# A gated feed-forward on one NeuronCore: the up-projection's 640 tokens split 512 + 128 over two PSUM banks, in place of 320 + 320

## The chip, the core and the metric

The kernel runs on one core of a Trainium2 chip. The metric is the device time of one execution in microseconds, lower is better. A core has TensorE (PE, with a matmul part and a weight-load part, PEld, that overlap), VectorE (DVE), ScalarE (ACT), GpSimd (POOL) and SyncE (SP, which here only issues DMAs). Matmul results land in PSUM, which has 8 banks of 512 f32 values per partition; one matmul writes into one bank.

## The reference

The program is a two-layer streaming encoder over 512 prompt tokens and 8 running streams with 16 new tokens each, 640 tokens in all. After the attention part, each layer ends in a gated feed-forward:

```
def _conv_ffn(x, conv_hist, w_up, conv_w, conv_b, w_down):
    u = x @ w_up
    a, b = u[..., :D_FF], u[..., D_FF:]
    a_ext = jnp.concatenate([conv_hist.astype(a.dtype), a], axis=1)
    a_conv = lax.conv_general_dilated(a_ext, conv_w[:, None, :].astype(a.dtype), (1,), 'VALID',
                                      dimension_numbers=('NWC', 'WIO', 'NWC'),
                                      feature_group_count=D_FF) + conv_b
    h = jax.nn.gelu(a_conv, approximate=False) * b
    return h @ w_down, a_ext[:, -(CONV_W - 1):]
```

The model width is 1024, D_FF is 2816, and the convolution has 3 taps along time. The prompt starts with an empty history; each of the 8 streams has its own history of 2 rows, and returns its last 2 rows. So the convolution treats the 512 prompt tokens as one run and the 128 stream tokens as 8 runs of 16.

## The kernel before, in words

Features lie on the partitions and the T = 640 tokens on the free dimension (HT = 320 is half of them, SEQ = 512, TS = 128). All weights come as slabs of up to 2048 columns, two slabs in flight. Precision comes from a split of every operand into a rounded high part and a low part of the type float32r, and each product is three matmuls: high x high, low x high, high x low.

- SyncE loads a slab into `w_raw`. ScalarE rounds it to `w_hi` (line 551), GpSimd subtracts to get `w_lo` (line 471).
- TensorE works in numbered *jobs*. A job is one 128-feature output tile for all 640 tokens; it owns two PSUM banks, and four jobs are in flight (8 banks). `dense` (lines 1131 to 1149) is a job over `tiles` contraction tiles: for each tile and each of the three products, two matmuls with the same weights, one for each half of the tokens. `four` (lines 1158 to 1177) runs four jobs together, tile by tile, as the layer norm before it delivers `x_lo`; it is used at the head of the input projection and at the head of the up-projection. The matmuls are recorded at line 1147 (`dense`) and line 1174 (`four`), those of the helper `full` with plain f32 at line 1155.
- `up_half` (lines 1395 to 1401) is the up-projection: a loop over slabs, each with one job for a tile of `a` and one for the same tile of `b`. It runs 10 slabs after `four` took the first two, then `down_half` works off 12 tiles, then `up_half` runs the other 10 slabs, and the last down-projection follows, with the layer norm.
- ScalarE's `feed` (lines 691 to 711) copies an `a` tile from PSUM into `f_ext`, the prompt after two zero columns, and each stream after its two history columns, and saves the new history in `tail`. VectorE's `feed` (lines 1048 to 1067) does the three taps into `f_conv`, ScalarE the gelu, VectorE the product with the `b` tile in PSUM into `f_h`, and the two split the result into `hf_hi` and `hf_lo`, from which `down_half` reads.

The order is written out by hand for each engine; semaphores (`job_done`, `job_taken`, `whi_ready`, `wlo_ready`, `fh_lo_ready` and others) hold the engines together. The inner loop of `dense`:

```
for x, w in ((hi, wh), (lo, wh), (hi, wl)):
    for a in range(2):
        ins = MM(out_[:, a, :], w, x[:, t, a * HT:(a + 1) * HT],
                 start=t == 0 and w is wh and x is hi, stop=t == tiles - 1 and w is wl)
```

Of the kernel before, what the change touches and what calls it, by code (L numbers as in the profile page):

```python
# [28 lines left out]
ALU = mybir.AluOpType  # L29
ACT = mybir.ActivationFunctionType  # L30
# [3 lines left out]
DEPTH, D, SEQ, NREQ, TDEC, PAST, CHUNK, WINDOW = 2, 1024, 512, 8, 16, 512, 64, 128  # L34
TS = NREQ * TDEC
T = SEQ + TS
HT = T // 2
KD = D // P
# [29 lines left out]
S_UP1 = S_OUT + 4  # L68
# [11 lines left out]
J_UP1 = J_OUT + KD + 3  # L80
# [51 lines left out]
def build(nc, inp, out):  # L132
    ctx = ExitStack()
    with ctx:
# [4 lines left out]
        x_hi = sb("x_hi", [P, KD, T], F32R)  # L139
        x_lo = sb("x_lo", [P, KD, T], F32R)  # L140
# [8 lines left out]
        tail = sb("tail", [P, NF, (NREQ + 1) * (CW - 1)])  # L149
# [95 lines left out]
        f_ext = place("f_ext", 12 * T, [P, EXT + 2])  # L245
        f_conv = place("f_conv", 12 * T + EXT + 2, [P, EXT + 2])
        f_gelu = place("f_gelu", 12 * T + 2 * (EXT + 2), [P, EXT + 2])
        assert 3 * (EXT + 2) <= 4 * T
        hf_lo = place("hf_lo", 24 * T, [P, F1, T], F32R)
        f_h = place("f_h", 36 * T, [P, T])  # L250
# [6 lines left out]
        ps = ctx.enter_context(nc.psum_tensor("ps", [P, 8, 512], F32))  # L257
# [48 lines left out]
        def pair(n, parts=slice(0, P)):  # L306
            k = 2 * (n % 4)
            return ps[parts, k:k + 2, 0:HT]

        def flat(bank, n, parts=slice(0, P)):  # L310

# [26 lines left out]
        def row(t, j):  # L338

            if isinstance(j, int):  # L340
                return t[:, j, :]
            return t[:, bass.ds(j, 1), :].rearrange("p a n -> p (a n)")
# [186 lines left out]
        def _(act):  # L529
            A = act.activation  # L530
            for k in range(KD):
                act.wait_ge(x_loaded[k // 2], 16)
                A(x_hi[:, k, :], x_in[:, k, :], ACT.Copy).then_inc(xn_hi, 1)
                if k in (1, 3):
                    s = k // 2
# [5 lines left out]
            with act.Fori(0, DEPTH) as layer:  # L541
# [149 lines left out]
                def feed(j, k, jj, job0, n_first, ahead):  # L691

                    act.wait_ge(job_done, layer * NJ + JC + n_first + 2 * jj + 1)
                    act.wait_ge(conv_ready, layer * NF + j + 1)
                    ahead(k, (0,))
                    a = pair(job0)
                    A(f_ext[:, 2:2 + HT], a[:, 0, :], ACT.Copy)
                    A(f_ext[:, 2 + HT:2 + SEQ], a[:, 1, 0:SEQ - HT], ACT.Copy)
                    streams = f_ext[:, 2 + SEQ:EXT].rearrange("p (r n) -> p r n", r=NREQ)
                    A(streams[:, :, 2:], a[:, 1, SEQ - HT:].rearrange("p (r n) -> p r n", r=NREQ), ACT.Copy)  # L700
                    A(streams[:, :, 0:2], row4(hist, j), ACT.Copy)
                    A(row(tail, j)[:, 0:2], a[:, 1, SEQ - HT - 2:SEQ - HT], ACT.Copy)
                    A(row(tail, j)[:, 2:].rearrange("p (r n) -> p r n", r=NREQ),  # L703
                      a[:, 1, SEQ - HT:].rearrange("p (r n) -> p r n", r=NREQ)[:, :, TDEC - 2:], ACT.Copy
                      ).then_inc(ext_ready, 1)
                    act.wait_ge(conv_ready, layer * NF + j + 2)
                    act.wait_ge(fh_ready, layer * NF + j + 1)
                    A(f_gelu[:, 0:NC_], f_conv[:, 0:NC_], ACT.Gelu).then_inc(gelu_ready, 1)  # L708
                    ahead(k, (1,))
                    act.wait_ge(fh_ready, layer * NF + j + 2)  # L710
                    A(row(hf_hi, jj), f_h[:], ACT.Copy).then_inc(fh_hi_ready, 1)  # L711
# [32 lines left out]
        def _(dve):  # L744
# [13 lines left out]
            TT, TSC, STT = dve.tensor_tensor, dve.tensor_scalar, dve.scalar_tensor_tensor  # L758
# [10 lines left out]
            with dve.Fori(0, DEPTH) as layer:  # L769
# [19 lines left out]
                for q in range(4):  # L789
                    ins = TT(kr_r[32 * q:32 * q + 32, :], kr_t[:, 0, :], kr_t[:, 1, :], ALU.add)  # L790
# [47 lines left out]
                for k in range(2):  # L838
# [6 lines left out]
                    for q in range(4):  # L845
                        ins = dve.tensor_copy(q_rs[:, :, 4 * k + q, :],
                                              q_r[32 * q:32 * q + 32, k, SEQ:].rearrange("p (r n) -> p r n", r=NREQ))
# [199 lines left out]
                def feed(j, jj, job0, n_first):  # L1047
                    w = lambda c: vec[:, bass.ds(V_CW + c * NF + j, 1)]
                    dve.wait_ge(ext_ready, layer * NF + j + 1)
                    dve.sem_inc(job_taken, 1)  # L1050
                    link(TSC(f_conv[:, 0:NC_], f_ext[:, 2:EXT], w(2), vec[:, bass.ds(V_CB + j, 1)], ALU.mult, ALU.add))  # L1051
                    link(STT(f_conv[:, 0:NC_], f_ext[:, 1:EXT - 1], w(1), f_conv[:, 0:NC_], ALU.mult, ALU.add))
                    STT(f_conv[:, 0:NC_], f_ext[:, 0:EXT - 2], w(0), f_conv[:, 0:NC_], ALU.mult, ALU.add  # L1053
                        ).then_inc(conv_ready, 1)
                    dve.wait_ge(job_done, layer * NJ + JC + n_first + 2 * jj + 2)
                    dve.wait_ge(gelu_ready, layer * NF + j + 1)
                    up = pair(job0 + 1)
                    TT(f_h[:, 0:HT], up[:, 0, :], f_gelu[:, 0:HT], ALU.mult)
                    TT(f_h[:, HT:SEQ], up[:, 1, 0:SEQ - HT], f_gelu[:, HT:SEQ], ALU.mult)
                    link(TT(f_h[:, SEQ:].rearrange("p (r n) -> p r n", r=NREQ),  # L1060
                            up[:, 1, SEQ - HT:].rearrange("p (r n) -> p r n", r=NREQ),
                            f_gelu[:, SEQ + 2:EXT].rearrange("p (r n) -> p r n", r=NREQ)[:, :, 0:TDEC], ALU.mult))
                    dve.sem_inc(fh_ready, 1)
                    dve.sem_inc(job_taken, 1)
                    dve.wait_ge(fh_hi_ready, layer * NF + j + 1)
                    TT(row(hf_lo, jj), f_h[:], row(hf_hi, jj).bitcast(F32), ALU.subtract).then_inc(fh_lo_ready, 1)  # L1066
                    dve.wait_ge(fh_lo_ready, layer * NF + j + 1)
# [41 lines left out]
        def _(pe):  # L1109
            MM = pe.matmul  # L1110
# [6 lines left out]
            with pe.Fori(0, DEPTH) as layer:  # L1117
# [9 lines left out]
                    pe.wait_ge(whi_ready, layer * (2 * NS) + (2 * s + half + 1) + i * (2 * sper))  # L1127
                    pe.wait_ge(wlo_ready, layer * (2 * NS) + (2 * s + half + 1) + i * (2 * sper))

                def dense(n, s, tile0, tiles, hi, lo, part=None, i=0, jper=0, sper=0, ready=None):  # L1130

                    start_job(n, i, jper)
                    if part is not None:
                        weights(s, part % 2, i, sper)
                    out_ = pair(n)
                    for t in range(tiles):
                        if part == 2 and t == tiles // 2:
                            weights(s, 1, i, sper)  # L1140
                        if ready is not None:
                            ready(t)
                        c = (tile0 + t) * P
                        wh, wl = w_hi[:, s % 2, c:c + P], w_lo[:, s % 2, c:c + P]
                        for x, w in ((hi, wh), (lo, wh), (hi, wl)):
                            for a in range(2):
                                ins = MM(out_[:, a, :], w, x[:, t, a * HT:(a + 1) * HT],  # L1147
                                         start=t == 0 and w is wh and x is hi, stop=t == tiles - 1 and w is wl)
                    ins.then_inc(job_done, 1)

# [4 lines left out]
                        ins = MM(out_[:, a, :], lhs, rhs[:, a * HT:(a + 1) * HT], start=first, stop=last)  # L1155
                    return ins

                def four(n, s, before):

                    for k in range(4):
                        start_job(n + k)

                    for t, slot in [(0, 0)] + [(t + 1 - slot, slot) for t in range(KD - 1) for slot in (0, 1)] + [(KD - 1, 1)]:
                        pe.wait_ge(xn_lo, before + t + 1)
                        for j in (2 * slot, 2 * slot + 1):
                            if t == 0:
                                weights(s + slot, j % 2)
                            out_ = pair(n + j)
                            c = (j % 2 * KD + t) * P  # L1170
                            wh, wl = w_hi[:, slot, c:c + P], w_lo[:, slot, c:c + P]
                            for x, w in ((x_hi, wh), (x_lo, wh), (x_hi, wl)):
                                for a in range(2):
                                    ins = MM(out_[:, a, :], w, x[:, t, a * HT:(a + 1) * HT],  # L1174
                                             start=t == 0 and w is wh and x is x_hi, stop=t == KD - 1 and w is wl)
                            if t == KD - 1:
                                ins.then_inc(job_done, 1)
# [217 lines left out]
                def up_half(s0, job0, n):  # L1395
                    settle(pe)
                    with pe.Fori(0, n) as i:
                        for k in range(2):
                            g = dict(i=i, jper=4, sper=2)
                            dense(job0 + 2 * k, s0 + k, 0, KD, x_hi, x_lo, 0, **g)  # L1400
                            dense(job0 + 2 * k + 1, s0 + k, KD, KD, x_hi, x_lo, 1, **g)

                def rows(t, f0):
                    pe.wait_ge(fh_lo_ready, layer * NF + (f0 + t + 1))
# [5 lines left out]
                            dense(job0 + k, s0 + k, 0, nf, hf_hi, hf_lo, 2, i=i, jper=4, sper=4,  # L1410
                                  ready=(lambda t: rows(t, 0)) if k == 0 else None)

                four(J_UP1, S_UP1, layer * (2 * KD) + KD)
                up_half(S_UP1 + 2, J_UP1 + 4, F1 // 2 - 1)
                down_half(S_DN1, J_DN1, F1)
                up_half(S_UP2, J_UP2, F2 // 2)
# [147 lines left out]
```

## Time and profile before

| | us |
|---|---|
| median of 2 runs | 2218.32 (2212.05 and 2224.59) |
| span of the profiled execution, first to last instruction | 2210.7 |
| PE busy in it | 2066.8 (93%) |
| DVE, ACT, POOL busy | 974.5, 649.3, 679.4 |

### The profile page before, as it was taken

The page shows a single profiled execution, that of the slowest core. Times are in us where ns is not written, and L with a number is a line of the kernel's source. Part 1 is how long each engine was busy: PE and PEld are TensorE (multiplying, and loading weights), DVE is VectorE, ACT ScalarE, POOL GpSimd, SP SyncE. Part 2 cuts the span into 40 slices and gives each one's busy share as a digit, 9 for nine tenths or more (in the row PEclk, how much of TensorE's full clock was granted, in tenths as well). Part 3 has the DMA queues.
Part 4 walks back from the last instruction along what each step waited for, and adds up shares of the span by engine and source line. Part 5 has one row for each costly group of instructions (what it writes and reads, how often), then busy time and mean ns, then how long its engine had stood idle before and what let it go on. Part 6 is the DMA issues. An engine that isn't in the chain of part 4 may idle for free.

```text
span 2210.7 us, 33980 instructions
## 1 busy us (share of the span) xinstructions
PE 2066.8 (93%) x12730; PEld 1892.0 (86%) x12730; DVE 974.5 (44%) x1437; ACT 649.3 (29%) x1267; POOL 679.4 (31%) x328
## 2 busy tenths in 40 slices
PE   6888999999989999999989889999998999999993
PEld 5774666999979999999989557689997999999992
DVE  3457444221656432343364764532147544234336
ACT  2213223322235321332231232233322433123322
POOL 2320000233624334432732100013345333343265
PEclk9897589999989999999999777999999999999997
DMA  5220011122212212211231101102221121221121
GB/s 145 107 91 0 33 33 51 58 72 83 73 39 95 71 58 83 93 69 48 79 119 57 48 13 42 62 29 77 80 80 58 61 92 57 76 79 73 55 79 71
DMA packets 36662, 148.56 MB, mean 67 GB/s; under 512 B 6488, under 2 KB 11384, under 8 KB 28344
## 3 DMA queue, kind: packets, MB, share of 16 engines
q1 hardware_dynamic: 36568, 147.30, 19.7%
q8 instruction: 60, 0.98, 0.2%
q14 instruction: 34, 0.28, 0.0%
HBM read 141.34 MB, written 7.78 MB: 67 GB/s over the span
## 4 chain that ended last, share of the span: by engine, by line
PE 77%; issue 13%; POOL 5%; DVE 4%; ACT 1%; DMA 0%; POOLq 0%; SPq 0%; DVEq 0%; ACTq 0%
PE ps L1147 59%; POOL w_lo L471 4%; PE ps L1281 2%; PE ps L1261 2%; PE ps L1258 2%; PE ps L1323 2%; PE ps L1268 1%; PE ps L1313 1%; PE ps L1240 1%; PE ps L1267 1%; PE ps L1327 1%; POOL sum_sq L495 1%; PE ps L1260 1%; ACT probs L586 1%; PE ps L1318 0%
## 5 line engine op out<-in xcount | busy, mean ns | idle before, releaser
L471 POOL TENSOR_TENSOR w_lo<-w_raw,w_hi 128x1024 fp32r<-128x1024 f32 (+3 forms) x268 | 581.2, 2182 | 1509.9 <-ACT w_hi L551 1499.0
L1147 PE MATMUL ps<-x_hi,w_hi 128*128 128x320 f32 x2016 | 462.3, 311 | 27.2 <-POOL w_lo L471 27.2
L1147 PE MATMUL ps<-x_hi,w_lo 128*128 128x320 f32 x2016 | 461.1, 310 | 0.0
L1147 PE MATMUL ps<-x_lo,w_hi 128*128 128x320 f32 x2016 | 461.0, 310 | 0.0
L551 ACT ACTIVATE w_hi<-w_raw 128x1024 fp32r<-128x1024 f32 (+3 forms) x264 | 239.0, 924 | 526.7 <-PE ps L1147 500.8
L1147 PEld LDWEIGHTS ps<-x_hi,w_hi 128*128 128x128 f32 x2016 | 338.8, 189 | 29.2 <-ACT w_hi L551 21.4
L1147 PEld LDWEIGHTS ps<-x_lo,w_hi 128*128 128x128 f32 x2016 | 338.8, 189 | 0.0
L1147 PEld LDWEIGHTS ps<-x_hi,w_lo 128*128 128x128 f32 x2016 | 338.6, 189 | 0.0
L1051 DVE TENSOR_SCALAR f_conv<-f_ext,vec 128x656 f32<-128x656 f32 x44 | 66.2, 1506 | 226.9 <-ACT tail L703 224.1
L1147 PE MATMUL ps<-hf_hi,w_hi 128*128 128x320 f32 x704 | 160.8, 309 | 0.0
L1147 PE MATMUL ps<-hf_hi,w_lo 128*128 128x320 f32 x704 | 160.3, 308 | 0.0
L1147 PE MATMUL ps<-hf_lo,w_hi 128*128 128x320 f32 x704 | 160.3, 308 | 0.0
L1147 PEld LDWEIGHTS ps<-hf_hi,w_hi 128*128 128x128 f32 x704 | 117.6, 188 | 0.3
L1147 PEld LDWEIGHTS ps<-hf_hi,w_lo 128*128 128x128 f32 x704 | 117.6, 188 | 0.0
L1147 PEld LDWEIGHTS ps<-hf_lo,w_hi 128*128 128x128 f32 x704 | 117.6, 188 | 0.0
L1066 DVE TENSOR_TENSOR hf_lo<-f_h,hf_hi 128x640 f32 x44 | 83.1, 1889 | 46.5 <-ACT hf_hi L711 46.5
L1174 PE MATMUL ps<-x_hi,w_hi 128*128 128x320 f32 x256 | 62.9, 329 | 38.4 <-DVE x_lo L1000 30.0
L958 DVE TENSOR_TENSOR mix_b<-ps,gate_b 128x640 f32<-128x640 f32 x16 | 13.2, 824 | 155.7 <-PE ps L1147 155.7
L1174 PEld LDWEIGHTS ps<-x_hi,w_hi 128*128 128x128 f32 x256 | 46.0, 203 | 41.5 <-issue 40.2
L708 ACT ACTIVATE f_gelu<-f_conv 128x656 f32<-128x656 f32 x44 | 33.1, 752 | 162.4 <-DVE f_conv L1053 162.4
L1281 PEld LDWEIGHTS ps<-ident,probs 128*128 128x128 f32 (+1 forms) x384 | 49.4, 158 | 36.5 <-issue 17.8
L1281 PE MATMUL ps<-ident,probs 128*128 128x128 f32 (+1 forms) x384 | 70.7, 323 | 8.9 <-DVE probs L900 8.9
(215 smaller groups left out, 3052.9 us busy)
## 6 DMA issues: line engine op xcount, KB each, us to landing
w_raw<-in_slabs SPq DMA_DIRECT2D x64, 1024.0 KB, 4.8
w_raw<-in_slabs SPq DMA_DIRECT2D x52, 768.0 KB, 4.1
w_raw<-in_slabs SPq DMA_DIRECT2D x16, 640.0 KB, 3.8
ckvc<-in_ckvc SPq DMA_DIRECT2D x16, 256.0 KB, 2.6
ckvc_t<-in_ckvc_t SPq DMA_DIRECT2D x16, 256.0 KB, 2.8
x_in<-in_x_t SPq DMA_DIRECT2D x4, 640.0 KB, 8.6
out_y_t<-res SPq DMA_DIRECT2D x8, 320.0 KB, 2.1
bias_p<-bias_table SPq DMA_DIRECT2D x2, 1024.0 KB, 7.9
```

The costliest lines, as they stand in the source:

```text
L471: pool.tensor_tensor(w_lo[:, s % 2, c], w_raw[:, s % 2, c], w_hi[:, s % 2, c].bitcast(F32), ALU.subtract).then_inc(wlo_ready, 1)
L495: pool.tensor_tensor(sum_sq[:], sq[:, 0, :] if k == 1 else sum_sq[:], sq[:, k % 2, :], ALU.add).then_inc(added_sq, 1)
L551: A(w_hi[:, s % 2, c], w_raw[:, s % 2, c], ACT.Copy).then_inc(whi_ready, 1)
L708: A(f_gelu[:, 0:NC_], f_conv[:, 0:NC_], ACT.Gelu).then_inc(gelu_ready, 1)
L1051: link(TSC(f_conv[:, 0:NC_], f_ext[:, 2:EXT], w(2), vec[:, bass.ds(V_CB + j, 1)], ALU.mult, ALU.add))
L1066: TT(row(hf_lo, jj), f_h[:], row(hf_hi, jj).bitcast(F32), ALU.subtract).then_inc(fh_lo_ready, 1)
L1147: ins = MM(out_[:, a, :], w, x[:, t, a * HT:(a + 1) * HT], start=t == 0 and w is wh and x is hi, stop=t == tiles - 1 and w is wl)
L1174: ins = MM(out_[:, a, :], w, x[:, t, a * HT:(a + 1) * HT], start=t == 0 and w is wh and x is x_hi, stop=t == KD - 1 and w is wl)
L1258: MM(sc, q_lat[:, h, i * P:(i + 1) * P], ckv_t[:, 0:n], start=True, stop=False)
L1261: ins = MM(sc, q_r[hp, h // 4, i * P:(i + 1) * P], kr_r[hp, 0:n], start=False, stop=True)
L1281: return pe.transpose(ps[0:n, 4 + half, c:c + P], src, ident[:])
L1323: ins = MM(o[:, 0:2 * P], ckv_tok[:, k, :], pt[:, k * 256:(k + 1) * 256], start=k == 0, stop=k == i)
```

## The change

In the up-projection the two matmuls of a pair take columns 0 to 511 (the prompt) and 512 to 639 (the streams) of the tokens, each into the start of its own bank. All other stages that use `dense` and `four` keep the cut at 320. The engines that read the two banks then find the prompt whole in one bank: ScalarE copies it with one instruction in place of two, and VectorE multiplies it with one in place of two.

```diff
+        def banks(n):
+            return ps[:, 2 * (n % 4), :], ps[:, 2 * (n % 4) + 1, :]
...
-                    a = pair(job0)
-                    A(f_ext[:, 2:2 + HT], a[:, 0, :], ACT.Copy)
-                    A(f_ext[:, 2 + HT:2 + SEQ], a[:, 1, 0:SEQ - HT], ACT.Copy)
+                    prompt, new = banks(job0)
+                    A(f_ext[:, 2:2 + SEQ], prompt, ACT.Copy)
                     streams = f_ext[:, 2 + SEQ:EXT].rearrange("p (r n) -> p r n", r=NREQ)
-                    A(streams[:, :, 2:], a[:, 1, SEQ - HT:].rearrange("p (r n) -> p r n", r=NREQ), ACT.Copy)
+                    A(streams[:, :, 2:], new[:, 0:TS].rearrange("p (r n) -> p r n", r=NREQ), ACT.Copy)
                     A(streams[:, :, 0:2], row4(hist, j), ACT.Copy)
-                    A(row(tail, j)[:, 0:2], a[:, 1, SEQ - HT - 2:SEQ - HT], ACT.Copy)
+                    A(row(tail, j)[:, 0:2], prompt[:, SEQ - 2:], ACT.Copy)
...
-                    up = pair(job0 + 1)
-                    TT(f_h[:, 0:HT], up[:, 0, :], f_gelu[:, 0:HT], ALU.mult)
-                    TT(f_h[:, HT:SEQ], up[:, 1, 0:SEQ - HT], f_gelu[:, HT:SEQ], ALU.mult)
+                    prompt, new = banks(job0 + 1)
+                    TT(f_h[:, 0:SEQ], prompt, f_gelu[:, 0:SEQ], ALU.mult)
                     link(TT(f_h[:, SEQ:].rearrange("p (r n) -> p r n", r=NREQ),
-                            up[:, 1, SEQ - HT:].rearrange("p (r n) -> p r n", r=NREQ),
+                            new[:, 0:TS].rearrange("p (r n) -> p r n", r=NREQ),
...
-                def dense(n, s, tile0, tiles, hi, lo, part=None, i=0, jper=0, sper=0, ready=None):
+                def dense(n, s, tile0, tiles, hi, lo, part=None, i=0, jper=0, sper=0, ready=None, cut=HT):
...
-                            for a in range(2):
-                                ins = MM(out_[:, a, :], w, x[:, t, a * HT:(a + 1) * HT],
+                            for to, c0, c1 in ((out_[0], 0, cut), (out_[1], cut, T)):
+                                ins = MM(to[:, 0:c1 - c0], w, x[:, t, c0:c1],
...
-                            dense(job0 + 2 * k, s0 + k, 0, KD, x_hi, x_lo, 0, **g)
-                            dense(job0 + 2 * k + 1, s0 + k, KD, KD, x_hi, x_lo, 1, **g)
+                            dense(job0 + 2 * k, s0 + k, 0, KD, x_hi, x_lo, 0, cut=SEQ, **g)
+                            dense(job0 + 2 * k + 1, s0 + k, KD, KD, x_hi, x_lo, 1, cut=SEQ, **g)
...
-                four(J_UP1, S_UP1, layer * (2 * KD) + KD)
+                four(J_UP1, S_UP1, layer * (2 * KD) + KD, SEQ)
```

(`four` has the same edit in its inner loop as `dense`.)

No instruction changes its place among the others. PE at the start of the first `up_half` loop, before (`ps` is PSUM, then the moving and the stationary operand, partitions x columns, and how many such rows follow each other):

```order
L1147 MATMUL ps<-x_hi,w_hi 128x320 x2
L1147 MATMUL ps<-x_lo,w_hi 128x320 x2
L1147 MATMUL ps<-x_hi,w_lo 128x320 x2
L1147 MATMUL ps<-x_hi,w_hi 128x320 x2
L1147 MATMUL ps<-x_lo,w_hi 128x320 x2
```

And the same place in the changed kernel:

```order
L1148 MATMUL ps<-x_hi,w_hi 128x512
L1148 MATMUL ps<-x_hi,w_hi 128x128
L1148 MATMUL ps<-x_lo,w_hi 128x512
L1148 MATMUL ps<-x_lo,w_hi 128x128
L1148 MATMUL ps<-x_hi,w_lo 128x512
L1148 MATMUL ps<-x_hi,w_lo 128x128
```

Two equal matmuls have become a wide and a narrow one with the same weights; the next wide one has other weights or other tokens.

## Rows read from the trace of the kernel before

**Rows 1.** The page: busy time by engine, and the chain of waits.

```profile
PE 2066.8 (93%) x12730; PEld 1892.0 (86%) x12730; DVE 974.5 (44%) x1437; ACT 649.3 (29%) x1267; POOL 679.4 (31%) x328
...
PE 77%; issue 13%; POOL 5%; DVE 4%; ACT 1%; DMA 0%; POOLq 0%; SPq 0%; DVEq 0%; ACTq 0%
```

**Rows 2.** Windows: length, busy us and count by engine, clock, DMA; first up, down, last up.

```profile
core 0: us, PE busy (x) PEld busy (x) DVE busy (x) ACT busy (x) POOL busy (x), PEclk, DMA share, GB/s
...
661.00:801.90 140.90, 140.89 (x961) 140.90 (x962) 71.18 (x80) 59.54 (x119) 51.90 (x22) 1.00 0.22 77
801.90:886.40 84.50, 84.50 (x579) 84.50 (x578) 23.29 (x18) 13.08 (x16) 32.49 (x15) 1.00 0.25 81
...
1956.00:2097.00 141.00, 141.00 (x963) 141.00 (x962) 60.24 (x69) 44.42 (x101) 48.77 (x21) 1.00 0.19 67
```

**Rows 3.** Timeline inside an up loop, matmuls, then loads: start, length, engine, count.

```profile
1000.47 0.46 PE L1147 MATMUL ps<-x_hi,w_lo 128*128 128x320 f32 x2
1000.76 0.46 PE L1147 MATMUL ps<-x_hi,w_hi 128*128 128x320 f32 x2
...
1000.62 0.34 PEld L1147 LDWEIGHTS ps<-x_hi,w_hi 128*128 128x128 f32 x2
1000.91 0.34 PEld L1147 LDWEIGHTS ps<-x_lo,w_hi 128*128 128x128 f32 x2
```

**Rows 4.** Loads by form (busy, mean ns), then two unhindered pairs in the timeline.

```profile
L1147 PEld LDWEIGHTS ps<-x_hi,w_hi 128*128 128x128 f32 x2016 | 338.8, 189 | 29.2 <-ACT w_hi L551 21.4 <-issue 7.5
...
L1155 PEld LDWEIGHTS ps<-q_nope,ukp 128*128 128x128 f32 x64 | 11.9, 190 | 10.0 <-DVE q_lat L808 5.6
...
L1354 PEld LDWEIGHTS ps<-q_lat,uv 128*64 128x64 f32 x32 | 4.4, 137 | 2.4
...
314.24 0.30 PEld L1267 LDWEIGHTS ps<-ckv_t,q_lat 128*128 128x128 f32 x2 [0.76 <-issue]
...
385.70 0.19 PEld L1353 LDWEIGHTS ps<-q_lat,uv 128*64 128x64 f32 x2
```

**Rows 5.** Timeline of plain f32: 128-column matmuls with loads, and loads of 320-column ones.

```profile
325.64 0.97 PEld L1327 LDWEIGHTS ps<-probs_t,ckvc 128*128 128x128 f32 x8 [0.55 <-issue]
...
325.64 1.16 PE L1327 MATMUL ps<-probs_t,ckvc 128*128 128x128 f32 x8
...
616.47 1.00 PEld L1155 LDWEIGHTS ps<-sum_sq,ones 128*128 128x128 f32 x4
```

**Rows 6.** Timeline where an up loop and layer two's `four` stage start.

```profile
661.01 0.53 PE L1147 MATMUL ps<-x_hi,w_hi 128*128 128x320 f32 x2 [0.98 <-POOL w_lo L471]
...
1699.03 0.87 PE L1174 MATMUL ps<-x_hi,w_hi 128*128 128x320 f32 x2 [10.00 <-DVE x_lo L1000]
1699.70 0.73 PE L1174 MATMUL ps<-x_lo,w_hi 128*128 128x320 f32 x2
1700.23 0.73 PE L1174 MATMUL ps<-x_hi,w_lo 128*128 128x320 f32 x2
```

**Rows 7.** ScalarE's and VectorE's instructions by form (busy, mean ns).

```profile
L611 ACT ACTIVATE probs_t<-ps 128x512 f32<-128x512 f32 x36 | 21.3, 591 | 16.9 <-PE ps L1281 16.9
L697 ACT ACTIVATE f_ext<-ps 128x320 f32<-128x320 f32 x44 | 18.5, 420 | 0.0
...
L698 ACT ACTIVATE f_ext<-ps 128x192 f32<-128x192 f32 x44 | 14.3, 324 | 0.0
...
L1058 DVE TENSOR_TENSOR f_h<-ps,f_gelu 128x320 f32<-128x320 f32 x44 | 21.6, 492 | 47.1 <-ACT f_gelu L708 32.2 <-PE ps L1147 14.8
...
L1059 DVE TENSOR_TENSOR f_h<-ps,f_gelu 128x192 f32<-128x192 f32 x44 | 15.3, 347 | 0.0
...
L907 DVE COPY probs_t<-ps 128x512 f32<-128x512 f32 x20 | 13.8, 690 | 8.9 <-PE ps L1281 8.7
```

**Rows 8.** Groups of the down-projection's matmuls (idle before), and a wait of PE's.

```profile
L1147 PE MATMUL ps<-hf_hi,w_hi 128*128 128x320 f32 x704 | 160.8, 309 | 0.0
...
PE ps L1147 <- POOL w_lo L471: 27.2, 6, 19.3
```

More of the change, by code:

```diff
@@ L695, in feed @@
                     ahead(k, (0,))
-                    a = pair(job0)
-                    A(f_ext[:, 2:2 + HT], a[:, 0, :], ACT.Copy)
-                    A(f_ext[:, 2 + HT:2 + SEQ], a[:, 1, 0:SEQ - HT], ACT.Copy)
+                    prompt, new = banks(job0)
+                    A(f_ext[:, 2:2 + SEQ], prompt, ACT.Copy)
                     streams = f_ext[:, 2 + SEQ:EXT].rearrange("p (r n) -> p r n", r=NREQ)
-                    A(streams[:, :, 2:], a[:, 1, SEQ - HT:].rearrange("p (r n) -> p r n", r=NREQ), ACT.Copy)
+                    A(streams[:, :, 2:], new[:, 0:TS].rearrange("p (r n) -> p r n", r=NREQ), ACT.Copy)
                     A(streams[:, :, 0:2], row4(hist, j), ACT.Copy)
-                    A(row(tail, j)[:, 0:2], a[:, 1, SEQ - HT - 2:SEQ - HT], ACT.Copy)
+                    A(row(tail, j)[:, 0:2], prompt[:, SEQ - 2:], ACT.Copy)
                     A(row(tail, j)[:, 2:].rearrange("p (r n) -> p r n", r=NREQ),
-                      a[:, 1, SEQ - HT:].rearrange("p (r n) -> p r n", r=NREQ)[:, :, TDEC - 2:], ACT.Copy
+                      new[:, 0:TS].rearrange("p (r n) -> p r n", r=NREQ)[:, :, TDEC - 2:], ACT.Copy
                       ).then_inc(ext_ready, 1)
@@ L1136, in dense @@
                         weights(s, part % 2, i, sper)
-                    out_ = pair(n)
+                    out_ = banks(n)
                     for t in range(tiles):
@@ L1156, in full, with four @@
                     return ins
-                def four(n, s, before):
+                def four(n, s, before, cut=HT):
                     for k in range(4):
@@ L1168, in four @@
                                 weights(s + slot, j % 2)
-                            out_ = pair(n + j)
+                            out_ = banks(n + j)
                             c = (j % 2 * KD + t) * P
@@ L1172, in four @@
                             for x, w in ((x_hi, wh), (x_lo, wh), (x_hi, wl)):
-                                for a in range(2):
-                                    ins = MM(out_[:, a, :], w, x[:, t, a * HT:(a + 1) * HT],
+                                for to, c0, c1 in ((out_[0], 0, cut), (out_[1], cut, T)):
+                                    ins = MM(to[:, 0:c1 - c0], w, x[:, t, c0:c1],
                                              start=t == 0 and w is wh and x is x_hi, stop=t == KD - 1 and w is wl)
```

## The prediction, made before the changed kernel ran

> **What bounds the kernel now.** I read the page first: PE is busy 93% of the span and holds 77% of the chain of waits, with line 1147 (the matmuls of `dense`) alone at 59%; VectorE, ScalarE and GpSimd stand at 44%, 29% and 31% [rows 1]. So I asked what PE does in the stages that the change touches. The windows view has the four loops of `up_half` (661.0 to 801.9, 886.4 to 1027.3, 1730.3 to 1871.2 and 1956.0 to 2097.0 us): PE is busy for the whole of each at a granted clock of 1.00, and it issues about 961 matmuls in 140.9 us [rows 2] (the first and the last of the four loops stand there, the others read the same). Each loop has 20 jobs of 8 tiles, 3 products and 2 matmuls, 960 in all, so one matmul costs 140.9 / 960 = 146.8 ns and a pair (the two matmuls that cover the 640 tokens) 293.5 ns. Nothing waits there, so whatever a pair gains or loses in these stages moves the end by the same amount.
>
> The timeline shows how a matmul and its weight load overlap: a pair of matmuls is recorded every 0.29 us, and beside it a pair of loads every 0.29 us [rows 3]. Each matmul has a load of its own, although both matmuls of a pair use the same weights. The records (about 310 ns a matmul, 188 a load) are latencies that overlap; the spacing is what counts. At 2.4 GHz (clock 1.00) and one column per cycle, 320 columns need 133.3 ns. The measured spacing is 13.5 ns more.
>
> **What a weight load costs.** This decides the case, since a 128-column matmul gives only 53.3 ns of streaming to hide the next load behind. Three readings agree:
> - Two loads of 128 columns that follow each other with nothing in their way take 0.30 us together; one record is 190 ns (the L1155 row), so the second starts 110 ns after the first. Two loads of 64 columns take 0.19 us, one record is 137 ns, so the second starts 53 ns after. The time goes with the columns of the weights, about 0.84 ns each [rows 4].
> - A load's record is this issue time plus some 82 ns of latency: 190 for 128 columns of plain f32, 137 for 64. The loads of the up-projection read 188 to 189, so they too occupy the loader for some 107 ns, although their type is the rounded f32 [rows 4].
> - The nearest place where loads of this size meet matmuls of 128 columns is line 1327: eight loads in 0.97 us, (0.97 - 0.19) / 7 = 111 ns apart, and the matmuls with them [rows 5]. There a plain-f32 matmul streams at two cycles a column (two records each, 107 ns), so stream and load are equal, and 111 is the price of a step whose load takes all of it.
>
> **The change, part by part.** (1) The *wide* matmul has 512 columns: 213.3 ns of stream plus the same 13.5 = 226.8 ns. Its load is hidden (107 < 213). (2) The *narrow* one has 128 columns, 53.3 ns of stream, 67 with the 13.5. But the load for the next wide matmul can start only when the narrow one has taken its own weights, as today each load starts with a matmul, one per step [rows 3]. So the step lasts as long as the load: 111 ns by [rows 5]. From below: 67 ns, if the load were hidden. From above: 147 ns, if today's 146.8 is no stream with a surcharge but already the load's own rhythm in this type; the trace has only 320-column matmuls of the type, so it can't tell the two apart. I take 111, since 107 of load fit well inside 147. (3) A pair then costs 226.8 + 111 = 337.8 ns against 293.5: +44.3 ns. The bytes, the products and the number of matmuls and loads stay the same.
>
> Pairs: 4 loops x 480 = 1920, and the two `four` stages at the head of the up-projection, 96 pairs each (192 matmuls at line 1174) = 192. 2112 x 44.3 ns = +93.6 us. In the `four` stages PE waits once for `x_lo` (10.0 us) before the first matmul and then runs on without a gap [rows 6], so these pairs count in full. The first few microseconds there run at half clock, with 0.27 us a matmul, the bare stream [rows 6]; a narrow step would cost two times 107 there, and the pair about +107 instead of +44. That is some 11 pairs a layer, 22 x 63 ns = +1.4 us. Sum: **+95 us**.
>
> (4) ScalarE's two copies of the prompt half into `f_ext` (420 + 324 ns) become one of 512 columns, nearest row 591 ns; VectorE's two products (492 + 347) become one, nearest row 690 ns [rows 7]. Some 0.15 us less on each engine, 44 times. I cost this at nothing: PE covers it, since the down-projection that waits for the last `hf_lo` starts with an idle time of 0.0 [rows 2, 8]. Were that cover gone, the gain would be at most 4 stage ends x 0.3 us. The remaining waits of PE near here, for `w_lo` of GpSimd (about 1 us at 661.0) [rows 6, 8], hang on the end of the `four` jobs and stay. Slabs, `w_hi` and `w_lo` get more time per job (8.1 us instead of 7.0) and fall no further behind. PSUM use is the same: a job still owns two banks, and no engine reads a bank before its job is done.
>
> **The numbers.** The profiled execution spans 2210.7 us; with +95 it would span 2306. The median of the runs shown, 2218.3, lies 7.6 us above that span, and I add the change to it: 2218 + 95 = **2313 us**. A measurement of this kernel tells about 2%, 44 us, from no change, that is 21 ns a pair.
>
> **Rivals.**
> - *Load as the rhythm of the type* (0.22): the 13.5 ns of today are part of the load. Wide 213.3 + 2.5 to 13.5, narrow 147: the pair is 363 to 374, +69 to +80 ns, +146 to +170 us: 2364 to 2388. For it: loads start with a matmul's start, and a plain-f32 matmul of 320 columns streams with only 2 ns over its cycles (four loads in 1.00 us are 270 ns apart, 640 cycles are 267) [rows 5], so something about this type costs more. Against it: at half clock the 13.5 vanish [rows 6], and the load should then be slower too.
> - *The load is hidden anyway* (0.08, the side of no change): if the rounded type loads faster than plain f32, the narrow step is 67 ns and the pair 293 again: 2218, or down to 2197 if the 13.5 ns were paid only once a pair. It decides as soon as a load takes under about 85 ns. Against it speak the records of 188 ns beside 190. [...]
> - *The narrow matmul falls back to the f32 pace* (0.10): this kernel's plain f32 matmuls take two records at two cycles a column, and at 128 columns that is 2 x 111 = 222 ns [rows 5]. If the rounded type keeps its fast pace only for wide operands, the pair is 449 ns, +155 ns, +328 us: 2546. No row has this type narrower than 320 columns, so nothing excludes it; for it speaks only that such a mode must have some condition.
> - *The clock* (0.02): the array is idle for a fifth of each pair (267 of 338 ns streaming). If the clock fell to half in these loops, the time would be above 2700. Against it: the short 128-column runs of the attention stage keep the pace of full clock [rows 5], and the half-clock stretches here stand behind waits of 10 us [rows 6].
>
> **Chances and range.** The main case, +95 with narrow steps of 100 to 125 ns, has 0.58 and gives 2281 to 2345 us (a pair of 323 to 353 ns). With the first rival the range from 2280 to 2395 holds 0.80; outside are 0.08 below and 0.12 far above. Slower by over 2%: 0.58 + 0.22 + 0.10 + 0.02, less 0.01 for a main case near its edge = 0.91. Within 2%: 0.08. Faster: 0.01.
>
> **What would show it.** In an up window of the new profile, matmuls of 512 and 128 columns should alternate with starts 227 and 111 ns apart, the loads with them, and a loop of 480 pairs should take 162 us instead of 140.9, with PE still without a gap and a clock of 1.00. The down stages must keep 146.8 ns a matmul. If narrow steps read 67, the load was hidden; 147, the load sets the rhythm; 220, the type has lost its pace. I am wrong in kind if the loops keep 140.9 us, and wrong in the sum if PE waits appear behind the up-projection.

## The result

The changed kernel takes 2301.4 us (median of 2295.5 and 2307.3) against 2218.3 before. The ratio of the two is 1.039, 95% interval 1.032 to 1.045. A larger comparison on another occasion gave 2310.0 us (median of 6 runs) against 2213.1 (17 runs), ratio 1.045, 1.040 to 1.049. So the change costs about 4%; the forecast was 2313 us, +95.

The profiled execution has a span of 2305.2 us, +94.5 against 2210.7. The windows view of the changed kernel has, in this order, the first `four` stage, the first up loop, the down-projection behind it, and the other three up loops; columns as in [rows 2]:

```profile
618.90:654.20 35.30, 35.01 (x193) 30.48 (x193) 16.55 (x21) 10.30 (x15) 2.39 (x1) 0.94 0.05 20
...
654.20:817.40 163.20, 163.20 (x960) 143.51 (x961) 71.40 (x69) 59.12 (x108) 51.47 (x22) 1.00 0.19 66
817.40:901.90 84.50, 84.50 (x578) 84.50 (x577) 23.38 (x17) 13.08 (x16) 32.68 (x15) 1.00 0.23 81
901.90:1065.10 163.20, 163.20 (x962) 143.96 (x961) 61.64 (x59) 44.27 (x90) 48.25 (x21) 1.00 0.17 59
1780.00:1943.20 163.20, 163.20 (x961) 143.61 (x961) 71.49 (x69) 59.14 (x108) 51.47 (x22) 1.00 0.19 66
2027.70:2190.90 163.20, 163.20 (x963) 143.78 (x961) 61.63 (x59) 44.27 (x90) 48.26 (x21) 1.00 0.16 59
```

Each up loop takes 163.2 us where it took 140.9 [rows 2], with the same 960 matmuls, the same clock of 1.00 and PE busy throughout. That is 340.0 ns a pair in place of 293.5. The down stage beside it keeps its 84.5 us. The loader's figure, the third in a row, is the new sign: the weight loader, busy without a break before (140.90), now has about 20 us a loop in which no load is recorded. A loader that waits while it is also the bottleneck sounds odd; the load timeline shows how both can be. Loads in an up loop after the change (start, length, engine, and so on, as in [rows 3]):

```profile
700.05 0.30 PEld L1148 LDWEIGHTS ps<-x_hi,w_hi 128*128 128x128 f32 x2
700.39 0.30 PEld L1148 LDWEIGHTS ps<-x_lo,w_hi 128*128 128x128 f32 x2
700.73 0.30 PEld L1148 LDWEIGHTS ps<-x_hi,w_lo 128*128 128x128 f32 x2
```

The loads now come in twos. Two of them need 0.30 us, and one record is 0.19, so the second starts 0.11 us after the first, like the unhindered pair of [rows 4]. Then comes a break, and the next two start 0.34 us after the last two. The reading that fits is this: the first load of a two begins when a narrow matmul begins to stream; the wide matmul behind it can't start without it, 0.11 us; it then streams for some 0.23 us, and the load for the narrow matmul after it is done long before that ends. In [rows 3] the loads came one per matmul, 0.147 us apart, each hidden. The exact starts in the trace are 108 and 232 ns apart in turn, in the first loop without exception; together they are the 340.

The matmul records of the same place read differently from what the prediction said they would (two lines of the timeline, each a wide matmul and the narrow one behind it, then two groups by form):

```profile
700.11 0.50 PE L1148 MATMUL ps<-x_hi,w_hi 128*128 128x512 f32 x2
700.45 0.50 PE L1148 MATMUL ps<-x_lo,w_hi 128*128 128x512 f32 x2
...
L1148 PE MATMUL ps<-x_lo,w_hi 128*128 128x512 f32 x640 | 283.1, 442 | 0.0
...
L1148 PE MATMUL ps<-x_lo,w_hi 128*128 128x128 f32 x640 | 142.5, 223 | 0.0
```

A wide record is 442 ns and a narrow one 223. The two together last 0.50 us, so the narrow one begins 0.28 us after the wide one, and the next wide one 0.06 us after that. Minus their stream (213 and 53 ns) the records leave 229 and 170 ns. The difference of 59 ns fits a record of the wide matmul that begins when the narrow one's stream ends, and so holds the time in which it waits for its weights. The matmul starts alone (60 and 280 ns apart) put the wait on the wide matmul, the loads on the narrow one. The sum is the same, and the experiments below show what it comes from.

The readers, by form (busy, mean ns), against [rows 7]:

```profile
L700 ACT ACTIVATE f_ext<-ps 128x512 f32<-128x512 f32 x44 | 25.6, 582 | 0.0
...
L1060 DVE TENSOR_TENSOR f_h<-ps,f_gelu 128x512 f32<-128x512 f32 x44 | 30.4, 692 | 78.0 <-PE ps L1148 67.2 <-ACT f_gelu L710 10.7
```

582 ns replace 420 + 324, and 692 replace 492 + 347. VectorE already waited for PE before this product (14.8 us in all) and now waits 67.2, so a shorter product can't move the end; a large part of the added wait is simply the slower PE.

### The profile page after: what moved, and what is told of

The parts are those of the page before. It is cut to its first block, busy times and chain, and to the rows that moved or that the text cites. A ratio compares the mean times of both kernels' runs of the same rounds, so it can differ in the third digit from the quotient of the medians.

```text
span 2305.2 us, 33892 instructions
## 1 busy us (share of the span) xinstructions
PE 2159.3 (94%) x12730; PEld 1900.5 (82%) x12730; DVE 978.7 (42%) x1393; ACT 648.3 (28%) x1223; POOL 678.1 (29%) x328
## 4 chain that ended last, share of the span: by engine, by line
PE 77%; issue 13%; POOL 5%; DVE 4%; ACT 1%; DMA 0%; POOLq 0%; SPq 0%; DVEq 0%; ACTq 0%
PE ps L1148 61%; POOL w_lo L474 4%; PE ps L1262 2%; PE ps L1282 2%; PE ps L1259 2%; PE ps L1324 2%; PE ps L1269 1%; PE ps L1268 1%; PE ps L1328 1%; ACT probs L589 1%; PE ps L1241 1%; PE ps L1314 1%; POOL sum_sq L498 1%; PE ps L1156 1%; PE ps L1261 1%
## 5 line engine op out<-in xcount | busy, mean ns | idle before, releaser
L1148 PE MATMUL ps<-x_hi,w_hi 128*128 128x512 f32 (+1 forms) x2016 | 491.3, 325 | 25.9 <-POOL w_lo L474 25.9
L1148 PE MATMUL ps<-x_lo,w_hi 128*128 128x512 f32 (+1 forms) x2016 | 490.3, 324 | 0.0
L1148 PE MATMUL ps<-x_hi,w_lo 128*128 128x512 f32 (+1 forms) x2016 | 490.2, 324 | 0.0
L1148 PEld LDWEIGHTS ps<-x_hi,w_hi 128*128 128x128 f32 x2016 | 315.5, 189 | 53.8 <-ACT w_hi L554 21.5
L1148 PEld LDWEIGHTS ps<-x_lo,w_hi 128*128 128x128 f32 x2016 | 315.6, 189 | 26.0
L1148 PEld LDWEIGHTS ps<-x_hi,w_lo 128*128 128x128 f32 x2016 | 315.5, 189 | 26.0
L1067 DVE TENSOR_TENSOR hf_lo<-f_h,hf_hi 128x640 f32 x44 | 89.5, 2035 | 46.5 <-ACT hf_hi L713 46.5
L1175 PE MATMUL ps<-x_hi,w_hi 128*128 128x320 f32 (+2 forms) x256 | 65.8, 340 | 38.5 <-DVE x_lo L1002 30.0
L1175 PEld LDWEIGHTS ps<-x_hi,w_hi 128*128 128x128 f32 x256 | 43.4, 202 | 44.7 <-issue 40.5
```

The lines of the kernel that those rows point to most:

```text
L1148: ins = MM(to[:, 0:c1 - c0], w, x[:, t, c0:c1], start=t == 0 and w is wh and x is hi, stop=t == tiles - 1 and w is wl)
L1175: ins = MM(to[:, 0:c1 - c0], w, x[:, t, c0:c1], start=t == 0 and w is wh and x is x_hi, stop=t == KD - 1 and w is wl)
```

## The experiments

In all of them only the up-projection differs. "Loop" is the length of an up loop in the run's windows view, the first one where nothing else is said, and a pair is that divided by 480.

**The change again, and its readers alone.** The first run is the changed kernel itself. The second splits its reads:

```diff
-                    A(f_ext[:, 2:2 + SEQ], prompt, ACT.Copy)
+                    A(f_ext[:, 2:2 + HT], prompt[:, 0:HT], ACT.Copy)
+                    A(f_ext[:, 2 + HT:2 + SEQ], prompt[:, HT:], ACT.Copy)
...
-                    TT(f_h[:, 0:SEQ], prompt, f_gelu[:, 0:SEQ], ALU.mult)
+                    TT(f_h[:, 0:HT], prompt[:, 0:HT], f_gelu[:, 0:HT], ALU.mult)
+                    TT(f_h[:, HT:SEQ], prompt[:, HT:], f_gelu[:, HT:SEQ], ALU.mult)
```

> The changed kernel once more, as the yardstick of this call. All theories: a pair of matmuls 340 ns, an up loop of 480 pairs 163.2 us, the whole about 3.9% over the kernel before.

> The matmuls as in the change (512 and 128 columns), but ScalarE and VectorE read the prompt in two instructions again (320 and 192 columns). Theory of the load (a narrow matmul waits for the next weight load): the readers are hidden, an up loop stays at 163.2 us and the time is that of the change within 0.3%. Rival, the readers count: the single read gave some 0.15 us back per tile and engine, and the time would be up to 7 us (44 x 0.15) above the change.

Measured: both have a ratio of 1.045 to the kernel before (1.040 to 1.049, and 1.039 to 1.050). The first loop of the change in the windows view:

```profile
657.40:820.60 163.20, 163.20 (x961) 143.62 (x961) 71.30 (x69) 59.10 (x108) 51.35 (x22) 1.00 0.19 66
```

And with the reads split:

```profile
665.50:828.70 163.20, 163.17 (x959) 143.52 (x960) 71.44 (x80) 59.82 (x119) 51.47 (x22) 1.00 0.19 66
```

VectorE has 80 instructions in place of 69 and ScalarE 119 in place of 108, and the stage is no longer. The readers are worth nothing here; the whole loss comes from the matmuls.

**The cut moved: 384, 396, 448.** `CUT` takes the place of SEQ as the boundary, and the readers take the prompt in two parts again:

```diff
+CUT = 384
...
-                            dense(job0 + 2 * k, s0 + k, 0, KD, x_hi, x_lo, 0, cut=SEQ, **g)
-                            dense(job0 + 2 * k + 1, s0 + k, KD, KD, x_hi, x_lo, 1, cut=SEQ, **g)
+                            dense(job0 + 2 * k, s0 + k, 0, KD, x_hi, x_lo, 0, cut=CUT, **g)
+                            dense(job0 + 2 * k + 1, s0 + k, KD, KD, x_hi, x_lo, 1, cut=CUT, **g)
```

> The cut at 384: matmuls of 384 and 256 columns. Theory of the load, a step lasts as long as the greater of columns/2.4 + 13.5 ns and about 112 ns: 173.5 + 120.2 = 293.7 ns a pair, an up loop 141.0 us, the time of the kernel before within 0.5%. Rival, the cost grows evenly with the difference of the two widths (320 and 320 cost 293.5, 512 and 128 cost 340): 309 ns a pair, 148.3 us a loop, +33 us.

> The cut at 396: matmuls of 396 and 244 columns, the narrow one still longer (244/2.4 + 13.4 = 115.1 ns) than the load's step of 113.3 ns, but under 256 columns. Theory of the load: 178.4 + 115.1 = 293.5 ns a pair, 140.9 us a loop, the time of the kernel before. Rival, the type loses its pace below 256 columns: at least 100 ns more a pair, 189 us a loop.

> The cut at 448: matmuls of 448 and 192 columns. Theory of the load: 200.2 + 112 (the load, since 192 columns give only 93.5) = 312 ns a pair, an up loop 149.9 us, +39 us (1.8%) against the kernel before. Rival, the cost grows evenly with the difference of the widths: 324.5 ns a pair, 155.8 us a loop, +65 us. Rival, the narrow type loses its pace below 256 columns (192 columns as slow as 128 in the change, or slower): 200 + at least 113 with no load needed, growing with the columns, 2 x 192/128: 370 ns, 177 us a loop.

Measured, ratio to the kernel before: 384 gave 1.000 (0.997 to 1.003), 396 gave 0.992 (0.988 to 0.997), 448 gave 1.021 (1.017 to 1.026), which is slower, but not clearly by 2%. The first loop with the cut at 384:

```profile
660.60:801.50 140.90, 140.90 (x961) 140.90 (x962) 71.01 (x80) 59.60 (x119) 51.60 (x22) 1.00 0.22 77
```

At 396:

```profile
659.60:798.90 139.30, 139.30 (x961) 139.30 (x962) 70.70 (x80) 59.31 (x119) 51.64 (x22) 1.00 0.22 78
```

At 448:

```profile
651.60:802.00 150.40, 150.40 (x960) 143.56 (x961) 71.41 (x80) 59.57 (x119) 51.68 (x22) 1.00 0.20 72
```

Read the busy times of PE and of the loader (the second and third figures) together: at 384 and 396 PE and the loader are both busy throughout, at 448 the loader begins to have breaks (143.56 of 150.40). The pair costs 293.5, 290.2 and 313.3 ns. A cost that grows evenly with the difference of the widths would have given 309 at 384 and 324.5 at 448; it falls. A pace that the type loses under 256 columns falls too: 244 columns cost nothing extra. What stands is a pair whose cost is nearly flat (290 to 293.5 ns) until the narrow stream is shorter than the load. At 448 it is 313.3 - (448/2.4 + 13.4) = 113.2 ns for the narrow step, where 112 was expected.

**The wide step alone.** Both matmuls get 512 columns; the second covers tokens 128 to 639, and columns 128 to 511 are computed twice:

```diff
-                            for to, c0, c1 in ((out_[0], 0, cut), (out_[1], cut, T)):
+                            for to, c0, c1 in ((out_[0], 0, cut), (out_[1], cut if cut == HT else T - SEQ, T)):
...
-                    A(streams[:, :, 2:], new[:, 0:TS].rearrange("p (r n) -> p r n", r=NREQ), ACT.Copy)
+                    A(streams[:, :, 2:], new[:, SEQ - TS:SEQ].rearrange("p (r n) -> p r n", r=NREQ), ACT.Copy)
```

> Both matmuls of a pair 512 columns wide, tokens 0 to 511 and 128 to 639; columns 128 to 511 are computed twice and the second copy is not read. This gives the wide step alone. Theory of the load, with 13.5 ns fixed on each matmul: 226.8 ns a step, 453.6 a pair, an up loop 217.7 us, about 2218 + 338 = 2556 us; the narrow step of the change is then 340 - 227 = 113. Rival, the 13.5 ns are 10% of the stream: 235 a step, 470 a pair, 225.6 us a loop, about 2590 us; the narrow step would then be 105. Rival, the narrow step is hidden at 60 and the wide one costs 280: 560 a pair, 269 us a loop, about 2780 us.

Measured: 2556.1 us (two runs), ratio 1.157 (1.143 to 1.172). The windows row of the first loop:

```profile
674.60:892.20 217.60, 217.60 (x961) 180.18 (x960) 70.75 (x68) 59.61 (x108) 51.23 (x22) 1.00 0.14 50
```

217.6 / 960 = 226.7 ns a wide step: 213.3 of stream and 13.4 on top, the same 13.4 as at 320 columns, so it does not grow with the columns. If the wide step keeps that length beside narrow ones, the narrow step of the change is 340.0 - 226.7 = **113.3 ns**. The starts of the loads in the changed kernel, 108 and 232 ns apart, would share out the same 340 otherwise: 108 for the load and 5 ns more on the wide step. No run settles how these 5 ns are shared; the sum is the same. The rival in which today's rhythm was the load's (147 ns) is out, since it needs a pair of 363 to 374 ns.

**Half and a quarter of the weight columns.** Each matmul of the up-projection takes 64 of the 128 weight columns (so half of the features are not computed), once with the cut of the change and once with 320 and 320; a third run takes 32 columns at 320 and 320 (three quarters not computed):

```diff
-                def dense(n, s, tile0, tiles, hi, lo, part=None, i=0, jper=0, sper=0, ready=None, cut=HT):
+                def dense(n, s, tile0, tiles, hi, lo, part=None, i=0, jper=0, sper=0, ready=None, cut=None):
...
-                            for to, c0, c1 in ((out_[0], 0, cut), (out_[1], cut, T)):
-                                ins = MM(to[:, 0:c1 - c0], w, x[:, t, c0:c1],
+                            for to, c0, c1 in ((out_[0], 0, cut or HT), (out_[1], cut or HT, T)):
+                                m = P if cut is None else P // 2
+                                ins = MM(to[0:m, 0:c1 - c0], w[:, 0:m], x[:, t, c0:c1],
```

(`cut` is given in the up-projection alone; the other stages keep all 128 weight columns. The third run has `P // 4`.)

> The change with 64 weight columns in place of 128 in every matmul of the up-projection: half of the features are not computed, the token columns stay 512 and 128. Theory of the load: a load takes half the time (about 54 ns), fits under the narrow stream, and a pair costs 227 + 67 = 294 ns or a little less, an up loop 141 us, the time of the kernel before. Rival, a 128-column matmul of this type costs 113 ns for its own shape: 340 ns a pair, 163.2 us a loop, the time of the change.

> The kernel before (320 and 320) with 64 weight columns in every matmul of the up-projection: half of the features are not computed. It asks where the 13.5 ns over the bare stream come from. If they come from the load that runs beside the stream and go with its columns: 140 ns a step, 280 a pair, 134.5 us a loop, -28 us. If they are fixed per matmul: 293.5 a pair, 140.9 us a loop, no change. If they are the rhythm of the load itself (147 ns for 128 columns): the step falls to the bare stream of 133.3 + 2.5 = 136, 272 a pair, 130.4 us a loop, -46 us.

> The kernel before (320 and 320) with 32 weight columns in every matmul of the up-projection: three quarters of the features are not computed. With 64 columns a loop kept its 140.8 us in three of four cases (138.7 in one). If the 13.4 ns over the stream have nothing to do with the load: again about 140.8 us. If they go with the load: 137 us or less.

Measured: 512 and 128 with 64 weight columns has a ratio of 0.996 to the kernel before (0.991 to 1.001), the kernel with 320 and 320 and 64 columns 0.997 (0.992 to 1.001), that with 32 columns 0.989 (0.972 to 1.005). The first loop of the 512/128 kernel with 64 weight columns:

```profile
662.10:801.30 139.20, 139.20 (x960) 93.32 (x961) 70.88 (x69) 58.65 (x108) 51.75 (x22) 1.00 0.22 78
```

The first two loops of the 320/320 kernel with 64:

```profile
660.90:799.60 138.70, 138.70 (x961) 129.34 (x962) 70.72 (x80) 59.22 (x119) 51.68 (x22) 1.00 0.22 78
884.00:1024.80 140.80, 140.80 (x962) 129.64 (x961) 59.88 (x68) 44.27 (x100) 48.63 (x21) 1.00 0.19 68
```

The first loop of the one with 32:

```profile
654.90:792.50 137.60, 137.58 (x960) 103.55 (x961) 70.88 (x80) 59.21 (x119) 51.78 (x22) 1.00 0.22 78
```

This is the test of the cause. The token columns are still 512 and 128, and the weights have half the columns: the pair falls from 340 to 290.0 ns. The edit shortens the load, and it also halves the output that each matmul writes (64 partitions in place of 128). The 320/320 run with the same halving is the control for that: three of its four loops stay as they were, and the first loses 2 us. At 128 token columns there is no such control, but the starts of the loads below show the gap itself shrinking with the load, from 0.11 to 0.06 us. So nearly all of the 50 ns come from the load. A 128-column matmul of this type is not slow in itself; it waited for the load. The loads in the timeline of the 512/128 run:

```profile
700.04 0.20 PEld L1149 LDWEIGHTS ps<-x_hi,w_lo 128*64 128x64 f32 x2
700.33 0.19 PEld L1149 LDWEIGHTS ps<-x_hi,w_hi 128*64 128x64 f32 x2
```

They still come in twos, but the two are only 0.06 us apart, as long as the narrow stream, and the next two follow after 0.29 us. The other two runs asked for the origin of the 13.4 ns. With 64 columns three of the four loops keep their 140.8 us and the first takes 138.7; with 32 all four take 137.6, 143.3 ns a step. So the greater part of the surcharge, 10 of 13.4 ns, stays when the weights have a quarter of the columns. It is mostly not the load, and what it is stays open.

**Another order.** For each tile the three wide matmuls first, then the three narrow ones; and the same order with 320 and 320:

```diff
-                        for x, w in ((hi, wh), (lo, wh), (hi, wl)):
-                            for to, c0, c1 in ((out_[0], 0, cut), (out_[1], cut, T)):
+                        sides, terms = ((out_[0], 0, cut), (out_[1], cut, T)), ((hi, wh), (lo, wh), (hi, wl))
+                        for (to, c0, c1), (x, w) in ([(p, q) for q in terms for p in sides] if cut == HT else
+                                                     [(p, q) for p in sides for q in terms]):
```

> The change with another order inside dense: for each tile the three wide matmuls first, then the three narrow ones, in place of wide and narrow in turn; weights, columns and products the same. Theory of the load: every narrow step is followed by a load that it can't hide, wherever it stands, so a pair stays at 340 ns and an up loop at 163.2 us. Rival, the excess comes from changing between wide and narrow or between the two banks: two changes a tile in place of six, a third of 46.5 ns, 309 ns a pair, 148.3 us a loop, +33 us against the kernel before.

> The kernel before (320 and 320) with the order of the grouped run in the up loops: for each tile the three matmuls of one bank, then the three of the other. The grouped 512/128 run gave 342 ns a pair in place of 340, with 232 ns between wide matmuls of the same bank, where two 512-column matmuls in alternating banks had given 226.7. If staying in one bank costs 5 ns: four of six steps at 152, two at 147, 150 ns on average, an up loop 144 us, +14 us in all. If not: 140.9 us a loop and no change.

Measured: ratio 1.049 (1.038 to 1.061) for 512 and 128, 1.000 (0.995 to 1.006) for 320 and 320. The first loop of 512 and 128 in this order:

```profile
658.30:822.50 164.20, 164.20 (x960) 143.71 (x961) 71.36 (x69) 59.12 (x108) 51.47 (x22) 1.00 0.19 66
```

And of 320 and 320:

```profile
661.30:802.10 140.80, 140.80 (x960) 140.80 (x961) 71.17 (x80) 59.52 (x119) 51.86 (x22) 1.00 0.22 77
```

Two changes of width a tile in place of six, and the loss is still there (342 ns a pair). In the timeline of the grouped 512/128 run the loads beside narrow matmuls stand 0.11 us apart, and those beside wide ones 0.23 to 0.24:

```profile
700.09 0.19 PEld L1149 LDWEIGHTS ps<-x_lo,w_hi 128*128 128x128 f32 x1
700.20 0.19 PEld L1149 LDWEIGHTS ps<-x_hi,w_lo 128*128 128x128 f32 x1
700.31 0.19 PEld L1149 LDWEIGHTS ps<-x_hi,w_hi 128*128 128x128 f32 x1
700.42 0.19 PEld L1149 LDWEIGHTS ps<-x_lo,w_hi 128*128 128x128 f32 x1
700.65 0.19 PEld L1149 LDWEIGHTS ps<-x_hi,w_lo 128*128 128x128 f32 x1
700.89 0.19 PEld L1149 LDWEIGHTS ps<-x_hi,w_hi 128*128 128x128 f32 x1
```

It is the narrow step that costs, wherever it stands. The extra 2 ns a pair are not explained: at 320 columns staying in one bank costs nothing, and 512 columns in one bank without narrow matmuls were not run.

## Why the prediction came out right

- **The bound.** PE without a gap at full clock was read correctly: 4 loops x (163.2 - 140.9) = +89.2 us of the +94.5 by which the span grew. The down stage kept its 84.5 us, as said, and the clock in the up loops its 1.00.
- **The wide step.** Said 226.8 ns, measured alone 226.7.
- **The narrow step.** Said 111 ns, from line 1327's plain-f32 row, with 67 and 147 as the bounds; it is 113.3 by difference, or 108 by the loads' starts with a wide step of 232. The row was not a clean source, since stream and load are equally long there (107 ns); the unhindered loads of [rows 4] and the run with half the weights carry the mechanism. The pair was 340.0 ns where 337.8 was said, 4.6 us over 2112 pairs.
- **The `four` stages.** Both kernels wait 10.0 us before them, as said. With the wait behind them, up to the first matmul of the loop, they take 35.3 and 35.8 us after the change. Before, they took 32.0 us (629.05 to 661.01) and 31.2 (from 1699.03 [rows 6] to 1730.3 [rows 2, 6]). The two together cost +7.9 us, where the sum had 8.5 for their pairs at full clock and 1.4 for the half-clock part. From first to last matmul the two stages grew by 9.4 us, close to that. At half clock the pairs start 0.64 us apart (at 619.56 and 620.20 us) in place of 0.53, 0.11 more, as said. What was wrong is the wait for `w_lo` behind them, which was to stay: it fell from 0.98 us [rows 6] to 0.29 in each layer. ScalarE and GpSimd need 4.8 us to make the next `w_hi` and `w_lo` in both kernels (656.05 to 660.86 us before, 649.21 to 654.03 after), while PE's last pairs beside them have become longer. The start of the first stage before, and the wait after:

```profile
629.05 0.87 PE L1174 MATMUL ps<-x_hi,w_hi 128*128 128x320 f32 x2 [10.00 <-DVE x_lo L1000]
...
654.18 0.53 PE L1148 MATMUL ps<-x_hi,w_hi 128*128 128x512 f32 x2 [0.29 <-POOL w_lo L474]
```

- **The sum.** 89.2 + 7.9 = +97.1 us by the stages, of which the span shows +94.5. The missing 2.6 us lie outside the changed stages. The attention stages of both layers, which no edit touches, took 243.4 and 234.9 us before, and 233.5 and 243.4 after, 1.4 us less in all; the other 1.2 us lie in stages not read here. The windows rows of the kernel after:

```profile
144.50:378.00 233.50, 211.47 (x935) 135.81 (x933) 135.44 (x369) 68.93 (x226) 3.98 (x2) 0.85 0.12 39
1259.80:1503.20 243.40, 225.17 (x934) 142.98 (x932) 135.57 (x369) 69.33 (x226) 3.97 (x2) 0.80 0.11 37
```

  The same instructions in two layers, 10 us apart, and the longer one has the lower granted clock (0.80 against 0.85); before it was 0.80 for the 243.4 us and 0.83 for the 234.9. One such shift is half a per cent of a run. The 17 runs of the unchanged kernel spread from 2202.5 us (mean clock 0.946) to 2231.5 (0.930). So the first difference of two medians, +83, each of two runs, is less good a measure of the change than the +97 of the larger comparison, and that the forecast of +95 lies within 2 us of the latter is in part luck.
- **The readers.** 582 and 692 ns, where 591 and 690 were taken from neighbours; costed at nothing; with the reads split again the loop stays at 163.2 us.
- **The rivals.** The rhythm of the type (147 ns) fell with the pair of 340, where it needs 363 to 374, and with the wide step alone; the hidden load with the pair of 340; the f32 pace with 290 ns at half the weight columns and with 244 columns at no cost; the clock with the 1.00 of all four up loops. Two numbers of the prediction don't follow from its own terms: 13.5 ns paid once a pair give 2190 us, not 2197, and narrow steps of 100 to 125 ns give pairs of 327 to 352 ns, not 323 to 353. Neither enters the sum. The Trainium skill, page "TensorE: Matmul & The Clock Gate", section "Weight-path perf modes — Fast Weight Load (FWL) and DoubleRow", has a fast load for 128 weights of an input type other than FP32, 4 times as fast in theory for fp8 and about 2 times as measured. No such load shows for this type here: two loads start 0.11 us apart, the same as in plain f32 [rows 4].
- **What it said would show it.** The signs "starts 227 and 111 apart" failed as a way of reading: matmul starts are 60 and 280 apart, since a matmul's record here holds its wait for the weights. By the prediction's own wording ("if narrow steps read 67, the load was hidden") a reader could have drawn the wrong conclusion from the first gap. The loads' starts (108 and 232) come nearer, and a run with one width gives the step of that width.

## What to carry to other kernels

Price a matmul step as the longer of two things: its own stream with its surcharge, and the weight load of the next one (here 113 ns for 128 weight columns, the same beside 512 and beside 448 token columns). Splitting a fixed number of columns unevenly is free until the shorter part falls below that, and from there each narrow matmul pays the difference. Here 244 columns were free and 192 were not; (113.3 - 13.4) x 2.4 puts the edge at an estimated 240. Read the margin off the profile beforehand: the loader's spacing where nothing hinders it, against the columns over the clock. Every matmul here loads its weights, also the narrow one, whose weights the wide one before it has just used; whether that load can be left out was not tried.

## What was not expected

- Each matmul of this type at full clock costs 13.4 ns over its columns at 2.4 GHz, the same at 320 and 512 columns, where plain f32 costs some 3 by the loads of [rows 5]. 10 ns of it stay when the load is a quarter as long. At half clock it is gone [rows 6]. Where it comes from is open.
- The surcharge has steps of its own. With 396 and 244 columns a pair costs 290 ns, not 293.5, in all four loops, and so does the pair of 512 and 128 with half the weights. It makes the cut at 396 the fastest of the versions that compute everything: 2208.6 us against 2220.6, ratio 0.992 (0.988 to 0.997). The loops account for 4 x 1.6 = 6.4 us of the 12; the rest is not explained. It beats both kernels, the one before by less than the 2% that counts as a difference here, and it reads the prompt in two parts, as the kernel before does.
- A wide step beside narrow ones is some 5 ns longer by its loads' starts than one among wide ones alone: 0.23 to 0.24 us in the grouped order, 0.232 in the order of the change, 0.227 with both matmuls at 512. Since the change alternates its banks and shows it too, the bank is not the reason. No run explains it.
